# Both layers' modulation made by TensorE in the first stage, and a re-ordered start of the expert search

## What is computed

```
def _layer(x, cond, p, ck, cv, cstate):
    mod = jax.nn.silu(cond) @ p['w_mod'] + p['b_mod']
    sh1, sc1, g1, sh2, sc2, g2 = jnp.split(mod, N_MOD, axis=-1)
    h = _rms(x, p['norm1']) * (1.0 + sc1) + sh1
    out, ctx = _token_mixers(h, p, ck, cv, cstate)
    x = x + g1 * out
    h = _rms(x, p['norm2']) * (1.0 + sc2) + sh2
    x = x + g2 * _peer(h, p)
    return x, ctx
def _peer(h, p):
    ...
    sv, si = lax.top_k(s, PEER_TOPK)
    cand = (sv[:, :, 0, :, None] + sv[:, :, 1, None, :]).reshape(...)
    top_s, top_j = lax.top_k(cand, PEER_TOPK)
    eidx = jnp.take_along_axis(cidx, top_j, axis=-1)
    g = jax.nn.softmax(top_s, axis=-1).astype(h.dtype)
    ...
        act = jax.nn.gelu(jnp.einsum('ced,cd->ce', u_tab[ei], xi))
        return jnp.einsum('ce,ced->cd', gi * act, v_tab[ei])
```

## Time and profile before

| | us |
|---|---|
| median of 3 runs (4712.84 to 4718.31) | 4716.57 |
| the profiled execution | 4705.3 |
| its span, first to last instruction | 4703.5 |
| TensorE busy | 4278.5 (91%) |
| DVE busy | 3423.5 (73%) |
| POOL busy | 2305.5 (49%) |
| ACT busy | 1959.4 (42%) |
| mean granted TensorE clock | 0.957 of full speed |

### The profile page before, as it was taken

How to read it: one execution, slowest core, us unless ns; L and a number is a source line. 1 busy time by engine, 2 the same in 40 slices (tenths; PEclk the granted TensorE clock), 3 DMA queues, 4 the chain that set the end, 5 groups by cost and what they waited for, 6 DMA issues and landing times. The chain is left out here.

```text
span 4703.5 us, 87292 instructions
## 1 busy us (share of the span) xinstructions
PE 4278.5 (91%) x34974; PEld 3853.6 (82%) x34974; DVE 3423.5 (73%) x6055; ACT 1959.4 (42%) x3469; POOL 2305.5 (49%) x1324
## 2 busy tenths in 40 slices
PE   7988888989999989989989888889899999999999
PEld 3866778988889878888878677779788898899998
DVE  6546555987674479999995566558876754799887
ACT  5434322246677422222225353322466774333332
POOL 0001131366677777777750011213566767777665
PEclk8989999999999999999999899999999999999999
DMA  7110011258999989999961100112589999999997
GB/s 302 59 49 12 4 75 68 93 188 278 308 320 339 356 325 345 346 347 347 346 242 54 53 12 4 75 64 88 180 278 302 321 338 350 333 371 371 364 362 278
DMA packets 388788, 1052.25 MB, mean 224 GB/s; under 512 B 32812, under 2 KB 183724, under 8 KB 384488
## 3 DMA queue, kind: packets, MB, share of 16 engines
q1 hardware_dynamic: 277864, 644.98, 38.0%
q0 software_dynamic: 110592, 402.70, 24.1%
HBM read 912.55 MB, written 135.00 MB: 223 GB/s over the span
## 5 line engine op out<-in xcount | busy, mean ns | idle before, releaser
L2353 POOL TENSOR_TENSOR tk_u_lo<-tk_u_raw,tk_u_hi 128x1024 fp32r<-128x1024 f32 x256 | 642.9, 2512 | 439.6 <-ACT tk_u_hi L2248 414.8
L1896 PE MATMUL ex_ps<-ex_wa_hi,ex_v_hi 128*128 128x448 f32 x2048 | 766.9, 374 | 87.6 <-DVE ex_wa_lo L2536 81.3
L1896 PE MATMUL ex_ps<-tk_h_hi,tk_u_hi 128*128 128x448 f32 x2048 | 784.2, 383 | 62.1 <-POOL tk_u_lo L2353 56.1
L1896 PE MATMUL ex_ps<-ex_wa_lo,ex_v_hi 128*128 128x448 f32 x2048 | 760.6, 371 | 0.0
L1896 PE MATMUL ex_ps<-ex_wa_hi,ex_v_lo 128*128 128x448 f32 x2048 | 759.9, 371 | 0.0
L1896 PE MATMUL ex_ps<-tk_h_hi,tk_u_lo 128*128 128x448 f32 x2048 | 757.7, 370 | 0.0
L1896 PE MATMUL ex_ps<-tk_h_lo,tk_u_hi 128*128 128x448 f32 x2048 | 757.6, 370 | 0.0
L2367 POOL TENSOR_TENSOR ex_v_lo<-ex_v_raw,ex_v_hi 128x1024 fp32r<-128x1024 f32 x160 | 439.4, 2747 | 304.5 <-ACT ex_v_hi L2284 304.0
L1896 PEld LDWEIGHTS ex_ps<-ex_wa_hi,ex_v_hi 128*128 128x128 f32 x2048 | 393.1, 192 | 138.5 <-DVE ex_wa_lo L2536 98.9
L2362 POOL DMA_INDIRECT tk_fetched<-in_expert_v,tk_picked x330 | 451.6, 1368 | 79.6 <-issue 66.6
L1896 PEld LDWEIGHTS ex_ps<-tk_h_hi,tk_u_hi 128*128 128x128 f32 x2048 | 391.9, 191 | 105.5 <-POOL tk_u_lo L2353 70.6
(11 more groups left out here) (370 smaller groups left out, 8592.6 us busy)
## 6 DMA issues: line engine op xcount, KB each, us to landing
tk_u_raw<-in_expert_u SPq DMA_DIRECT2D x256, 512.0 KB, 5.7
ex_v_raw<-in_expert_v SPq DMA_DIRECT2D x256, 512.0 KB, 6.5
act_spill<-tk_act_e SPq DMA_DIRECT2D x256, 224.0 KB, 4.5
grid_scratch<-tk_grid SPq DMA_DIRECT2D x112, 512.0 KB, 6.8
ex_a<-act_spill SPq DMA_DIRECT2D x64, 896.0 KB, 7.5
ex_g<-grid_scratch SPq DMA_DIRECT2D x64, 896.0 KB, 10.4
mod_w<-in_w_mod SPq DMA_DIRECT2D x12, 2048.0 KB, 9.3
ex_w_mod<-in_w_mod_rows SPq DMA_DIRECT2D x48, 512.0 KB, 5.8
```

What stands on the lines that cost most here:

```text
L1896: ins = nc.tensor.matmul(out, a, b, start=(first and n == 0), stop=(last and n == 2))
L2353: nc.gpsimd.tensor_tensor(u_lo[:, r % 2], u_raw[:, r % 3], u_hi[:, r % 2].bitcast(F32), ALU.subtract).then_inc(e["u_split"], 1)
```

## The change

1. `prologue` makes both layers' modulation: N goes from 12 to 24 loads, in the same loop. The part of layer 1 is put in `mod_sums` at the end. `cond_rows`, the tanh on rows and `silu_rows` are gone.
2. `experts` of layer 0 loses `modulate`, `load_m`, the read of `silu_rows` and SP's wait for 192 dots; `POOL_LOW` is (1, 3) in both layers.
3. In both layers, DVE searches tile 1 first (all of it but `keep`) where it searched the context, and the context in the first four chunks where it searched tile 1; `keep` of tile 1 stays in the fourth chunk. TensorE's `turn(2)` moves from before chunk 3 to before chunk 1.
4. POOL's wait for the context's picks goes from before the chunks to the first fetch that needs them (number 32).
5. The first four chunks take 3 dots each instead of 4, so 42 dots are late instead of 38.

```
-    N = 48 // CH
+    N = LAYERS * 48 // CH
...
-                sp.dma_start(crow[:], s.d["cond_rows"]).then_inc(e["crow_in"], 16)
...
-                    if n == 6:
-                        sp.wait_ge(e["crow_ready"], 1)
-                        sp.dma_start(s.d["silu_rows"], crow[:]).then_inc(e["crow_out"], 16)
...
-                low(0)
-                low(1)
-                low(2)
-                dve.wait_ge(e["tanhed_r"], 1)
-                link(nc.vector.tensor_scalar(tanh_r[:], tanh_r[:], 0.5, 0.5, ALU.mult, ALU.add))
-                nc.vector.tensor_tensor(crow[:], crow[:], tanh_r[:], ALU.mult).then_inc(e["crow_ready"], 1)
-                for n in range(3, N):
+                for n in range(N):
                     low(n)
...
+                nc.vector.tensor_copy(s.mod_sums[:], parts[:, 48:96, 1, :])
...
+                link(nc.vector.tensor_tensor(s.mod_sums[:], s.mod_sums[:], parts[:, 48:96, 0, :], ALU.add))
...
-    POOL_LOW = (1, 2, 3) if modulate_next else (1, 3)
+    POOL_LOW = (1, 3)
...
-        bounds.append(bounds[-1] + (4 if c < FIRST_CHUNKS else 5 + c % 2))
+        bounds.append(bounds[-1] + (3 if c < FIRST_CHUNKS else 5 + c % 2))
...
-                if modulate_next:
-                    sp.wait_ge(e["dotted"], JOBS)
-                    sp.dma_start(silu[:], s.d["silu_rows"]).then_inc(e["silu_in"], 16)
-                    load_m(0)
-                    load_m(1)
...
-                    if c == FIRST_CHUNKS - 1:
+                    if c == 1:
                         turn(2)
...
                 def fetch(n):
                     k, of = n % U, n % JOBS
+                    if n == CTX_JOBS.start:
+                        pool.wait_ge(e["picked"], 2)
...
-                pool.wait_ge(e["picked"], 2)
...
                     def ranks():
+                        if place == 2:
+                            dve.wait_ge(e["turned"], 2)
...
-                        dve.wait_ge(e["turned"], place if place else 1)
+                        dve.wait_ge(e["turned"], 1 if place == 0 else max(place, 2))
...
-                for n, part in enumerate(search(0, 1)):
+                first_tile, context = search(1, 1), search(0, 2)
+                for n, part in enumerate(first_tile[:-1]):
                     part()
                     if n < EARLY_DOTS:
                         dot(n)
...
-                        if c == 0:
-                            parts = search(1, 2)
-                        for n in (2 * c, 2 * c + 1):
-                            if n == CHUNKS - 1:
-                                dve.wait_ge(e["hot"], c + 1)
-                            parts[n]()
+                        for part in context[2 * c:2 * c + 2]:
+                            part()
+                        if c == FIRST_CHUNKS - 1:
+                            dve.wait_ge(e["hot"], c + 1)
+                            first_tile[-1]()
...
-                    for n in blocks_modulated(r):
-                        modulate(n)
```

More of the change, by code:

```diff
@@ L128, in prologue @@
         ps = mem.enter_context(nc.psum_tensor("mod_ps", [4, U, W], F32))
-        ps_t = mem.enter_context(nc.psum_tensor("mod_ps_t", [P, 48 * 4], F32))
-        names = ["cond_in", "ident_in", "pv_in", "crow_in", "x_in", "const_in", "w_in0", "w_in1", "w_in2", "tanhed", "tanhed_r",
-                 "silu", "crow_ready", "crow_out", "hi", "split", "done", "rows_ready", "turned", "chain"]
+        ps_t = mem.enter_context(nc.psum_tensor("mod_ps_t", [P, LAYERS * 48 * 4], F32))
+        names = ["cond_in", "ident_in", "pv_in", "x_in", "const_in", "w_in0", "w_in1", "w_in2", "tanhed",
+                 "silu", "hi", "split", "done", "rows_ready", "turned", "chain"]
         with stage(nc, *["p_" + n for n in names]) as (block, *sems):
@@ L179, in _ @@
                 high(1)
-                act.wait_ge(e["crow_in"], 16)
-                nc.scalar.activation(tanh_r[:], crow[:], ACT.Tanh, scale=0.5).then_inc(e["tanhed_r"], 1)
                 for n in range(N):
@@ L1996, in experts @@
         a1 = sb("a1", [P, A, DENSE])
-        sb("spare", [P, 1280])
-        silu, w_mod, spent = sb("silu", [P, 2, D]), sb("w_mod", [P, 2, D]), sb("spent", [P, D])
+        sb("spare", [P, 6400])
         g1 = sb("g1", [P, HALVES, A, BLOCK])
@@ L2026, in experts @@
             row_in = [e["row%d" % k] for k in range(U)]
-            v_in, ag_in, m_in = [e["v_in%d" % k] for k in range(R)], (e["ag_in0"], e["ag_in1"]), (e["m_in0"], e["m_in1"])
-            def blocks_modulated(r):
-                return [] if not modulate_next or r < 4 else [n for n in ((r - 4) * 2 // 5,) if (r - 4) * 2 % 5 in (0, 1) and n < 48]
+            v_in, ag_in = [e["v_in%d" % k] for k in range(R)], (e["ag_in0"], e["ag_in1"])
             def wait_low(eng, turn, r):
@@ L2548, in add_row @@
                                                ALU.mult, ALU.add).then_inc(e["summed"], 1)
-                def modulate(n):
-                    dve.wait_ge(m_in[n % 2], n // 2 * 16 + 16)
-                    if n == 0:
-                        dve.wait_ge(e["silu_in"], 16)
-                    for k in range(2):
-                        if 2 * n + k:
-                            dve.wait_ge(e["m_sum"], 2 * n + k)
-                        v.tensor_tensor_reduce(spent[:], w_mod[:, n % 2], silu[:, k], 1.0, 0.0, ALU.mult, ALU.add,
-                                               s.mod_sums[:, n, k:k + 1]).then_inc(e["m_sum"], 1)
                 late = Chain(dve, e["late"])
```

19 lines of the change are left out of this document (3 added, 16 removed).

## The result

Four runs of the changed kernel took 4644.48 to 4679.73 us, median **4660.5** against 4714.7 for the kernel before: ratio 0.9894, interval 0.9863 to 0.9926, or 50 us (35 to 65). Six more executions of it, beside eleven of the kernel before, gave 4659.9 and 0.9885 (0.9863 to 0.9907). The forecast was 4643 and -73 us: the direction held, the measured gain is a third smaller than the forecast one, and the ratio applied to the time before (4716.6 x 0.9894 = 4666.6) lies just over the range's end of 4664.

The account below looks back on a forecast made before the run. DVE was taken to bound layer 0's second half, TensorE layer 1's, no engine the first stage. Terms -113.7 + 55.3 - 22 + 7 = -73.4 us gave 4643 us; own range 4632 to 4655, 8-in-10 range 4628 to 4664.

Parts of the forecast that it names:

- The second half of layer 0: Layer 0's second `experts` half, freed of the modulation, becomes like layer 1's: -113.7 us (-117 to -108).
- Rival 5: Layer 0's second half is not freed as far as layer 1's, DVE setting the pace at some 650 us: 4664 us; chance 0.03.
- The first stage: The prologue makes 24 weight loads instead of 12, the added ones 5.3 us apart: together +55.3 us (+49 to +71).
- the rows of silu(cond): In the first stage, dropping their 1 MB load, two DVE operations and 1 MB store saves 8.8 us (0 to -9).
- Rival 2: The first stage runs at its best distance, 4.83 us per load, since nothing disturbs the loads: 4633 us; chance 0.08.
- The prediction's own sign of being wrong: In the first stage, ACT's splits under 4.9 or over 6 us apart would show the prediction wrong.
- the Trainium skill's faster pace: First stage: at about 436 GB/s a 2 MB load takes 4.8 us, the 24 costing 11 us less than forecast.
- The first chunks: In both layers' first chunks TensorE no longer waits before `turn(2)`: together -22 us (-26 to 0).
- chunk 3's one-hots: In the first chunks, they come 2.4 us sooner by two fewer dots, in time for TensorE by 2 us.
- Rival 1: The search's new order gains nothing in the first chunks, DVE's one-hots staying the last thing: 4665 us; chance 0.15.
- The meeting: Where the halves meet, four more late dots per layer cost +3.5 us each, together +7 us (0 to +18).
- Rival 3: Where the halves meet, the late dots cost their whole delay, 12 us per layer: 4660 us; chance 0.06.

Follow-up runs that it names:

- mod_only: The changed kernel with the search put back as before (four dots per first chunk, turn(2) at chunk 3): 4681.2 us, ratio 0.9934 to the kernel before.
- buf5: The changed kernel with five buffers instead of three for the first stage's loaded weights: 4643.9 us, ratio 0.9855 to the kernel before.
- dots4: The changed kernel with four dots in each first chunk instead of three: rows 0 to 32 take 200.8 and 200.9 us, the meetings of the halves 10.1.
- late36: The changed kernel with six dots instead of five in six later chunks, so 36 dots are late instead of 42: 4635.8 us in one execution.

## Why the prediction missed

**The second half of layer 0** (-113.7): right, -113.4 here and in mod_only (642.9 us). Taking layer 1's half as the picture, additions included, needed no model. Rival 5 (DVE still at its limit) is out.

**The first stage** (+55.3): the step that failed, and 16 of the 20 us. The prediction called the stage a loop through three buffers, which buf5 proved, and then priced the loop at "the shortest landing, 7.4 us": 15.4 / 3 = 5.1, and took 5.3 by the mean of four distances. But in the earlier trace rows 7.4 is the minimum; the median beside it is 9.3. With landings of over 9 us and loads issued some 5 to 6 us apart, the load before is still under way when the next is issued. (9.3 + 3.6 + 4.4) / 3 = 5.8, and 12 x 5.8 = 69 us. The twelve additional loads came 6.10 us apart, +73 instead of +63.6. The second error is the -8.8 us for the rows of silu(cond). The two long places did go (7.4 became 4.9, and 17.3 for two became 12.6), but the distances around them grew: after its pauses the old stage ran at 4.89, the new one at 5.1 to 6.8. Over the first eleven distances the old stage took 66.8 to 67.6 us in three executions and the new one, with its three buffers, 62.5 to 65.1 in seven: -3.0 in the mean, and -4.3 in this pair. In this pair the tail is 1.9 longer, and the start 0.5: 73.2 - 4.3 + 1.9 + 0.5 = +71.3. The simplest estimate, all eleven distances of the old stage (66.8 us, 6.07 each) taken for twelve more, gives +72.9. Rival 2 (4.83 us) was on the wrong side; the slow side of the term ended at 5.87 per load, just short of 5.90. The prediction's own sign of being wrong, splits over 6 us apart, did not show in the mean of all 24 (5.90), only in that of the twelve added ones.

The sentence on the Trainium skill's faster pace ("SBUF — State Buffer", section SBUF: two separate sides: an estimated 4.8 us at 436 GB/s) described a limit that the runs bear out, 4.89 us in three kernels, but one that this stage did not reach with three buffers.

**The first chunks** (-22): right in size, -22.5, and in where the large waits stand. The claim that chunk 3's one-hots come in time by 2 us was wrong, TensorE waits 0.2 us for them; and the forecast gave the fewer dots no other part, while dots4 shows that a quarter of the gain there (3.0 of 11.2 us per layer) is theirs, by way of chunk 2, and is paid back at the meeting. Rival 1 (nothing gained) is out.

**The meeting** (+7): +7.2, the right size from wrong parts. The forecast took 8 us lost at the first row of the second half, less part of the waits that followed. The waits of TensorE in layer 1 of the changed kernel, 3980 to 4002, then 4002 to 4050, answer:

```profile
PE ex_ps L1883 <- DVE ex_wa_lo L2508: 3.2, 1, 3.2
```

```profile
PE ex_ps L1883 <- DVE ex_wa_lo L2508: 3.8, 2, 2.2
PE ex_ps L1883 <- POOL ex_v_lo L2338: 2.4, 1, 2.4
```

The new wait is 3.2 us, not 8, and the waits behind it are 6.2 us in all, as before (6.3): nothing of them was saved. That the two errors cancel is luck. The late dots cost 3.6 us per layer, and dots4 and late36 both take nearly all of it back. Rival 3 (12 per layer) is out.

**What the sum had no term for**: the stretch from the first stage to layer 0's first gelu, +7.3 in this pair of executions and some 6 in the means of three and eleven executions; rows 32 to 125, +4.9 and -5.1, which is scatter. With +71 for the first stage and +6 for that stretch the sum is -52, and the two ratios say -50 and -54.

**The range**: the first stage's own bounds, +49 to +71, held the measured term, but the sum did not carry them. Of the 16 us between +55.3 and +71 the forecast's range took 7, those of the pace, and none for the chance that the rows of silu(cond) give nothing back. So its slow end was 4655, and 4664 came from the rivals, whose stories were others. It was the whole slow side of the first stage that came true, and some 5 us beside it.

## What to carry to other kernels

A loop through buffers is priced with the landing it has when it runs, the median beside the minimum, and a stage that is doubled is best costed by the whole of the stage that is there, disturbances included, before any of them is taken off. A DMA share near 1 does not say that the transfers are at their limit: look at the GB/s, and where another stretch moves more, more buffers may bring it, as two more did here. Work on POOL is not free for DVE: look at the mean time of DVE's smallest operation with and without it. And when TensorE shows busy without a gap, look at the distances between its starts before calling it undisturbed.
